# First normalisation of a two-block model: order of the loads, where the gain is applied, and how its tail interleaves with the first projections

## The reference, cut to what matters

```
h    = x * rsqrt(mean(x*x, axis=-1) + 1e-6) * attn_pre_norm     # x: 1024 x 1024
proj = h @ attn_w_in                                            # 1024 x 10240
bias = rel_bias[t5_bucket(...)]                                 # 32 x 16 table, three dilations
```

## Time and profile before

| what | value |
|---|---|
| median of 3 runs | 3475.45 us (3473.95 to 3476.17) |
| the profiled execution: its own time | 3471.2 us |
| its span, first to last instruction | 3469.0 us |
| TensorE busy, share of the span | 94% |
| VectorE, ScalarE, GpSimd busy | 43%, 33%, 31% |
| mean granted TensorE clock | 0.973 |

### The profile page before, as it was taken

One profiled execution on the slowest core, in us unless ns is written; L12 is line 12 of the kernel. 1 busy time (PEld: TensorE's weight loads), 2 busy tenths in 40 slices (PEclk: granted clock), 3 DMA queues, 4 the chain that ended last, 5 costly groups with the idle time before them and its releaser, 6 DMA issues. The chain is left out here.

```text
span 3469.0 us, 49092 instructions
## 1 busy us (share of the span) xinstructions
PE 3266.9 (94%) x19726; PEld 2605.1 (75%) x19726; DVE 1479.6 (43%) x3290; ACT 1131.0 (33%) x2453; POOL 1078.6 (31%) x541
## 2 busy tenths in 40 slices
PE   5999999999999999999999999999999899999997
PEld 4777778778787777778777777777787777777775
DVE  3253132221313236388133254455455724565554
ACT  4333434333332334321313222244342412144421
POOL 1356566222222242224332222211124122212241
PEclk8999999999999999999999999999999999999998
DMA  5313223343523323223623200101003310111113
GB/s 135 75 38 89 60 77 80 87 127 101 132 62 105 97 82 110 76 77 119 214 79 128 70 25 25 36 19 30 25 25 110 114 48 25 31 36 36 31 43 128
DMA packets 324517, 261.00 MB, mean 75 GB/s; under 512 B 75269, under 2 KB 288537, under 8 KB 324298
## 3 DMA queue, kind: packets, MB, share of 16 engines
q10 hardware_dynamic: 122156, 143.83, 13.7%
q1 hardware_dynamic: 202142, 114.09, 11.7%
HBM read 220.89 MB, written 48.58 MB: 78 GB/s over the span
## 5 line engine op out<-in xcount | busy, mean ns | idle before, releaser
L2458 POOL TENSOR_TENSOR w_hi<-w_raw,one 128x1024 fp32r<-128x1024 f32 x170 | 328.6, 1933 | 2108.8 <-PE psum L1434 1015.1
L2616 PE MATMUL psum<-act_hi,w_hi 128*128 128x512 f32 x1280 | 508.9, 398 | 31.6 <-ACT arena L1169 20.1
L1434 PE MATMUL psum<-act_hi,w_hi 128*128 128x512 f32 (+1 forms) x1376 | 511.7, 372 | 23.9 <-DVE arena L1907 13.1
L1434 PE MATMUL psum<-act_lo,w_hi 128*128 128x512 f32 (+1 forms) x1376 | 511.4, 372 | 0.0
L1434 PE MATMUL psum<-act_hi,w_lo 128*128 128x512 f32 (+1 forms) x1376 | 509.3, 370 | 0.0
L2616 PE MATMUL psum<-act_lo,w_hi 128*128 128x512 f32 x1280 | 509.0, 398 | 0.0
L2616 PE MATMUL psum<-act_hi,w_lo 128*128 128x512 f32 x1280 | 505.5, 395 | 0.0
L2461 POOL TENSOR_TENSOR w_lo<-w_raw,w_hi 128x1024 fp32r<-128x1024 f32 x170 | 432.2, 2542 | 13.3
L3364 DVE CUSTOM_DVE_ANT_0 arena<-psum,arena 128x128 f32<-128x128 f32 (+1 forms) x384 | 111.9, 347 | 506.2 <-PE psum L2655 337.6
L1434 PEld LDWEIGHTS psum<-act_hi,w_hi 128*128 128x128 f32 x1376 | 261.4, 190 | 74.6 <-DVE arena L1907 15.1
L2616 PEld LDWEIGHTS psum<-act_hi,w_hi 128*128 128x128 f32 x1280 | 242.4, 189 | 90.1 <-ACT arena L1169 22.2
(11 more groups left out here) (369 smaller groups left out, 5337.8 us busy)
## 6 DMA issues: line engine op xcount, KB each, us to landing
w_raw<-in_attn_w_in SPq DMA_DIRECT2D x80, 512.0 KB, 3.8
w_raw<-in_w_in SPq DMA_DIRECT2D x64, 512.0 KB, 4.0
spare<-in_w_mod ACTq DMA_DIRECT2D x24, 1024.0 KB, 7.9
x<-arena ACTq DMA_DIRECT2D x24, 512.0 KB, 2.9
arena<-x ACTq DMA_DIRECT2D x24, 512.0 KB, 4.4
arena<-in_x ACTq DMA_DIRECT2D x16, 512.0 KB, 5.1
arena<-weight_rows ACTq DMA_DIRECT2D x16, 512.0 KB, 6.4
w_raw<-in_ssm_w_in SPq DMA_DIRECT2D x16, 512.0 KB, 3.7
```

The lines of the kernel that those rows point to most:

```text
L1434: ins = nc.tensor.matmul(psum[:, n % 2, 0:c], w[:, slot % 2, k * P:(k + 1) * P], a[:, k, c0:c0 + c], start=(m == 0), stop=(m == 23))
L2458: G.tensor_tensor(w_hi[:, par], w_raw[:, par], one[:, 0:1].to_broadcast([P, 1024]), ALU.mult).then_inc(slot_hi, 1)
L2616: ins = nc.tensor.matmul(psum[:, h % 2, :], w[:, (3 + j) % 2, k * P:(k + 1) * P], a[:, k, c:c + 512], start=(m == 0), stop=(m == 23))
```

## The change

What it does, part by part:

1. ACT issues the first row tile before any constant, then `ident`, the gain, tile 1, `rel_bias`, `onehot`, tiles 2 and 3 in one DMA, tiles 4 and 5 in one, and after the statistics of tile 0 tiles 6 and 7 in one. All eight tiles have a buffer. An extra square root on a constant comes ahead of the first statistics.
2. The gain is loaded as a row spread over 128 partitions (512 KB), and DVE applies it with the scaling of the rows, in one instruction with two tensor inputs.
3. The turned tile is taken from PSUM directly: ACT rounds it to the high part, DVE subtracts for the low part. L255 and L290 are gone. The turned tiles lie in banks 4 to 7, the bias products in banks 0 to 2.
4. PE turns tiles 0 and 1, makes the bias products, turns tiles 2 to 4, and then puts 8 matmuls of half h = 14 ahead of each of tiles 5, 6 and 7. Then come h = 16, h = 15, and h = 17, 18, 19. The meeting of the engines is replaced by marks without a wait, and by PE's waits on `t_lo`.
5. DVE copies the bias products after scaling tile 2. SP's spread starts on that copy.
6. ACT takes out h = 14 and h = 16 ahead of `k_mat` and the bias loads. The two `c` loads, and their SiLU, are moved from the start to here: the loads behind the bias loads and ahead of the evacuations of h = 15, 17, 18 and 19, the SiLU behind those.

```diff
+        T_ROWS = region(4096, 8, 1024)
+        def start_act(act):
...
+            load(0, 1, 0)
+            act.dma_start(ident[:, :], io["c_ident"]).then_inc(const_loaded, 16)
+            act.dma_start(T_GAIN, spread_rows(io["attn_pre_norm"][0])).then_inc(const_loaded, 16)
+            load(1, 1, 1)
+            act.dma_start(relb[0:32, :], io["rel_bias"]).then_inc(const_loaded, 16)
+            act.dma_start(onehot[0:33, :], io["c_onehot"]).then_inc(const_loaded, 16)
+            load(2, 2, 2)
+            load(4, 2, 3)
+            act.wait_ge(one_set, 3)
+            nc.scalar.activation(T_STAT[:, 0, 1:2], one[:, 0:1], ACT.Sqrt)
+            stats(0)
+            load(6, 2, 0)
+            for t in range(NT):
+                if t + 1 < NT:
+                    stats(t + 1)
+                act.wait_ge(t_turned, t + 1)
+                nc.scalar.copy(act_hi[:, :, t * P:(t + 1) * P], T_PS(t % 2).rearrange("p (k c) -> p k c", k=KT)).then_inc(t_hi, 1)
...
+                if t == 0:
+                    dve.wait_ge(const_loaded, 16 * 4)
+                if t >= 2:
+                    dve.wait_ge(t_turned, t - 1)
+                nc.vector.scalar_tensor_tensor(T_NORM[:, b], T_ROWS[:, t], T_STAT[:, b, 3:4], T_GAIN,
+                                               ALU.mult, ALU.mult).then_inc(t_scaled, 1)
+            scale(0)
+            for t in range(NT):
+                if t + 1 < NT:
                     scale(t + 1)
+                if t == 1:
+                    dve.wait_ge(b_spread, 1)
+                    nc.vector.tensor_copy(spread[0:16, :, :], psum[0:16, 0:3, 0:384]).then_inc(b_copied, 1)
+                dve.wait_ge(t_hi, t + 1)
...
+                nc.vector.tensor_tensor(act_lo[:, :, cols], T_PS(t % 2).rearrange("p (k c) -> p k c", k=KT),
                                         act_hi[:, :, cols].bitcast(F32), ALU.subtract).then_inc(t_lo, 1)
...
@@ PE
             pe.wait_ge(const_loaded, 16 * 4)
+            turn_first(pe, 0)
+            turn_first(pe, 1)
...
-            t_pe(pe, 0, NT, True)
-            stage_end(pe, 1)
+            for t in range(2, 5):
+                turn_first(pe, t)
...
-            proj(-1, 14, 0, 144)
+            pe.wait_ge(b_copied, 2)
+            pe.wait_ge(t_lo, 4)
+            for i in range(3):
+                proj(-1, 14, 8 * i, 8 * i + 8)
+                turn_first(pe, 5 + i)
+            proj(-1, 14, 48, 72)
+            pe.wait_ge(t_lo, NT)
+            stage_mark(pe)
+            proj(-1, 14, 24, 48)
+            proj(-1, 14, 72, 144)
@@ ACT
+            evac(-1, 14, 0)
+            evac(-1, 16, 0)
             act.wait_ge(c_zero, 3)
             act.dma_start(k_mat[:, :, 0:P], ...).then_inc(k_stored, 16)
             act.wait_ge(b_skewed, 48)
             for g in ORDER:
                 load_bias(0, g)
-            for h in range(14, 20):
+            for i, name in enumerate(("c_2", "c_ctx_2")):
+                ...
+                act.dma_start(c_cols[:, :, i], v.rearrange("(k p) -> p k", p=P), allow_slow_non_contiguous=True).then_inc(m_c, 16)
+            for h in (15, 17, 18, 19):
                 evac(-1, h, 0)
+            act.wait_ge(m_c, 32)
+            nc.scalar.activation(c_cols[:, :, :], c_cols[:, :, :], ACT.Silu).then_inc(m_c, 1)
```

More of the change, by code:

```diff
@@ L221, in t_act @@
[L221 to L227, removed]
-            def stats(t):
[L230 to L237, removed]
+        T_ROWS = region(4096, 8, 1024)
@@ new lines, in build, with load @@
+        T_NORM = region(12288, 2, 1024)
+        T_GAIN = region(17408, 1024)
+        T_JUNK = region(18432, 1024)
+        T_STAT = region(19456, 2, 4)
+        def start_act(act):
+            tiles = x_in.rearrange("(t p) d -> p t d", p=P)
+            def load(t, n, sem_at):
+                act.dma_start(T_ROWS[:, t:t + n], tiles[:, t:t + n]).then_inc(t_loaded[sem_at], 16)
+            def stats(t):
+                b = t % 2
+                if t in (0, 1, 2, 4, 6):
+                    act.wait_ge(t_loaded[(0, 1, 2, 0, 3, 0, 0)[t]], 32 if t == 6 else 16)
+                if t >= 2:
+                    act.wait_ge(t_rstd, t - 1)
+                nc.scalar.activation(T_JUNK, T_ROWS[:, t], ACT.Square, accum_out=T_STAT[:, b, 0:1]).then_inc(t_square, 1)
+                act.wait_ge(t_square, t + 1)
@@ L238, in stats @@
                 nc.scalar.activation(T_STAT[:, b, 2:3], T_STAT[:, b, 0:1], ACT.Sqrt, scale=1.0 / D,
                                      bias=rms_eps[:, 0:1]).then_inc(t_root, 1)
[L241 to L249, removed]
-                    stats(t + 1)
[L251 to L264, removed]
@@ L266, in t_dve @@
-        def t_dve(dve, base, tiles, norm, gain, dst0):
+            load(0, 1, 0)
[6 more added lines that the diff above has]
+            load(4, 2, 3)
@@ new lines, in start_act @@
+            act.wait_ge(one_set, 3)
[4 more added lines that the diff above has]
+                if t + 1 < NT:
+                    stats(t + 1)
+                act.wait_ge(t_turned, t + 1)
+                nc.scalar.copy(act_hi[:, :, t * P:(t + 1) * P], T_PS(t % 2).rearrange("p (k c) -> p k c", k=KT)).then_inc(t_hi, 1)
+            for i in range(1, 4):
+                act.sem_inc(t_loaded[i], 16)
@@ L268, in scale, with start_dve @@
+            act.sem_inc(t_full_act, NT)
+        def start_dve(dve):
             def scale(t):
[L269 to L271 removed]
+                b = t % 2
+                dve.wait_ge(t_root, t + 1)
                 nc.vector.reciprocal(T_STAT[:, b, 3:4], T_STAT[:, b, 2:3]).then_inc(t_rstd, 1)
[L273 to L284, removed]
-                    scale(t + 1)
[L286 to L296, removed]
+                dve.wait_ge(t_rstd, t + 1)
@@ L297, in t_dve @@
                                         act_hi[:, :, cols].bitcast(F32), ALU.subtract).then_inc(t_lo, 1)
+            dve.sem_inc(t_full_dve, NT)
         def T_PS(b):
[L300 to L317, removed]
+            return psum[:, 4 + 2 * b:6 + 2 * b, :].rearrange("p a c -> p (a c)")
@@ L320, in build, with turn_first @@
+        def turn_first(pe, t):
+            pe.wait_ge(t_scaled, t + 1)
+            if t >= 2:
+                pe.wait_ge(t_lo, t - 1)
+            for k in range(KT):
+                ins = nc.tensor.transpose(T_PS(t % 2)[:, k * P:(k + 1) * P], T_NORM[:, t % 2, k * P:(k + 1) * P], ident[:, :])
+            ins.then_inc(t_turned, 1)
         PASSES = ((w_hi, act_hi), (w_hi, act_lo), (w_lo, act_hi))
@@ L2862, in _ @@
         def _(act):
[L2864 to L2875, removed]
             act.sem_inc(g_evac[0], 1)
             act.sem_inc(g_evac[1], 1)
+            start_act(act)
+            stage_mark(act)
             def load_bias(hp, g):
@@ L3337, in _ @@
             nc.vector.memset(relb[32:33, :], NEG).then_inc(b_copied, 1)
[L3338 to L3342, removed]
+            start_dve(dve)
+            stage_mark(dve)
             nc.vector.memset(BIAS[0:64, :, 576:640], NEG).then_inc(c_zero, 1)
```

18 lines of the change are left out of this document (5 added, 13 removed).

## The result

The changed kernel takes 3479.21 us (median of 20 runs, 3470.45 to 3483.97), the kernel before 3473.64 us (20 runs, 3465.44 to 3480.28). The ratio is 1.0016, 95% interval 1.0009 to 1.0023: the change costs 5.6 us (3.1 to 8.0). That is slower by 0.16%, under the 0.2% that the prediction called no change, though the interval reaches 0.23%. It is 2.2 us above the 3477.0 forecast and inside its range. The forecast stood on a kernel before of 3475.45 us (three runs); against the 3473.64 of twenty, its change of +1.5 us is to be held beside 5.6. The profiled execution took 3479.56 us, with a span of 3477.8 us and a mean granted clock of 0.972.

A forecast was written before the change was run, and what follows sets the result against it. SyncE's list, with two chokes ahead of slot 3, was taken to bound the prologue. +0.9 and +0.6 gave +1.5 us, 3471.2 to 3472.7 profiled; with the median 4.25 above, 3477.0 us, range 3472 to 3486.

The forecast's parts named there:

- The mechanism: In the prologue, SyncE's list sets the end; the norm's gain becomes a longer wait for slot 3; no change, chance 0.62.
- the head start: TensorE, after the faster norm, is 15 to 20 us ahead near 52 us; costed at nothing because slot 3 hides it.
- the chokes: Two stretches with DMA engines 5% busy, each during one `ssm_log_dt` load; forecast at 46 to 63 and 72 to 87.
- The sum: Whole prologue: +0.9 us at the first choke's start plus +0.6 for the `c` loads, together +1.5 us.
- The bias copy: DVE's copy of the bias products, which SyncE's spread awaits, ends at 20.6 us, 6.6 later (4.7 to 7.8).
- scaling tile 2 and the low part of tile 0 ... are done by 16, under the products: On DVE, both stand ahead of the bias copy but finish by 16 us, during the bias products.
- The spread no longer sharing: Row tiles 4 to 7 no longer share the DMA engines with SyncE's bias spread, saving 5.7 us.
- The `c` loads: Their 2048 single elements fall between the chokes or behind the second, costing slot 3 0 to 2 us, taken as 0.6.
- The restart: After TensorE's gap before slot 3 the clock is low as before; the longer gap changes nothing.
- the cover: TensorE finishes its sixth half near 90 us and slot 3 is ready at 96 to 97, leaving 6 to 7 us.
- The rival that put it behind the second choke: ScalarE's second `c` load is held until 86.0 us, delaying h = 15; 8.8 us lost, 3484.3 us; chance 0.28.
- The full head start: With neither ACT's queue nor slot 3 in the way, h = 17 to 19 end near 70; 26 us faster, 3449; chance 0.02.

The follow-up runs named there:

- only the late spread: Kernel before, with SyncE waiting for the high part of tile 0 before issuing the bias spread; 3478.28 us (12 runs), ratio 1.0023.
- the run with the late loads: Changed kernel, with the two `c` loads moved behind the last evacuation, h = 19; 3476.01 us (11 runs), ratio 1.0011 to the kernel before.

## Why the prediction was right, and where it was not

**The mechanism held.** SyncE's list set the end, the head start went into a longer wait for slot 3 (11.83 us, forecast longer than 5.7), the chokes lie at 46 to 64 and 73 to 88 (forecast 46 to 63 and 72 to 87), the first projection at 28.30 (forecast 28), and slot 3 is multiplied at 99.96 (forecast 97.5). TensorE was through with h = 15 at 52.84 (forecast 52). The sum was +1.5 us, with bounds of -1.3 and +4.5, and is +4.67 at the front: no change beyond 0.2% was right, the size at the front short by 3 us. That 3477.0 came within 2.2 us of the median is in part luck, since the kernel before that it was built on was 1.8 us above the median of twenty runs. The terms below are differences taken one behind the other along one path of two profiles, so they add up by construction, and a miss of 1 us in one of them is no more than two profiles of one code differ by. Term by term:

*The bias copy: +6.6 forecast, +7.3 measured.* It ends at 21.35. The constants were in at 12.0, not 10.5. DVE and TensorE around the copy:

```profile
12.02 1.28 DVE L263 SCALAR_TENSOR_TENSOR arena<-arena 128x1024 f32<-128x1024 f32 x1 [3.94 <-DMA arena<-c_onehot]
...
18.04 2.05 DVE L263 SCALAR_TENSOR_TENSOR arena<-arena 128x1024 f32<-128x1024 f32 x1
20.01 1.34 DVE L272 COPY arena<-psum 16x1152 f32<-16x1152 f32 x1
```

```profile
16.66 2.10 PE L2573 MATMUL psum<-arena 33*16 33x384 f32 x6
```

The products took 2.10 us, not 4.02, and were done at 18.76. The step that said "scaling tile 2 and the low part of tile 0 ... are done by 16, under the products" was wrong: the low part starts at 16.47, scaling tile 2 at 18.04, and the copy waits for that, not for the products. That the copy still ended only 0.7 us late is luck: the constants were 1.5 us later and DVE's order cost 1.25, and the products gave 1.9 back. The scaling itself took 2.05 us there, beside GpSimd's split of slot 1:

```profile
17.11 1.89 POOL L2430 TENSOR_TENSOR w_hi<-w_raw,one 128x1024 fp32r<-128x1024 f32 x1 [5.81 <-DMA w_raw<-in_attn_w_in]
19.09 3.23 POOL L2433 TENSOR_TENSOR w_lo<-w_raw,w_hi 128x1024 fp32r<-128x1024 f32 x1
```

Alone the two take 1.28 and 2.34 us. The Trainium skill, "SBUF — State Buffer", section "SBUF: two separate sides", says that a DVE instruction with two inputs in SBUF and a GpSimd instruction that reads SBUF exclude each other for the whole instruction. By that rule the scaling would run from 19.00 to 20.28; the trace has it end at 20.09. The low part would run from then for 2.34 us, to 22.43; it ends at 22.32. The trace agrees with the rule.

*The spread no longer sharing: -5.7 forecast, -4.4 measured.* The copy is 7.3 us later and the first `ssm_log_dt` lands 2.9 us later (66.92 against 64.01). This is the largest miss, 1.3 us, and it may be none: from the spread's first issue to that of the first `ssm_log_dt` it is 28.3 us before and 23.5 after, but 22.2 to 22.9 in the four other profiles that are the same up to there, which would be 5.4 to 6.1 us saved. The size forecast lies between.

*The `c` loads: +0.6 forecast, their cost not shown.* From the landing of the first `ssm_log_dt` to the split of slot 3 it is 28.6 us, before 27.6, and this +1.0 is what the sum needs. But with the two loads moved away it is 28.7, and in the kernel before with only the late spread, where no `c` load stands there, 28.1. What makes up the +1.0 is open.

*The restart: nothing forecast, +0.8 measured.* The clock is at 0.50 after both gaps; the step "the new gap is longer and ends the same way, so nothing changes" was wrong, four more matmuls ran slow. The length of the gap is not what did it: behind a gap of 5.29 us, in the run with only the late spread, eleven ran slow too.

The sum: 7.3 - 4.4 + 1.0 + 0.8 = 4.7 us. The norm's groups answer to the earlier trace rows:

```profile
L263 DVE SCALAR_TENSOR_TENSOR arena<-arena 128x1024 f32<-128x1024 f32 x8 | 11.0, 1380 | 4.2 <-DMA arena<-c_onehot 3.9
L275 DVE TENSOR_TENSOR act_lo<-psum,act_hi 128x1024 fp32r<-128x1024 f32 x8 | 9.8, 1219 | 4.5 <-ACT act_hi L247 4.5
```

The scaling took 1380 ns in the mean where 1.23 us were taken (1.28 but for the one beside GpSimd), and the subtraction 1219, as forecast.

**ScalarE.** It was free at 68.05 (forecast 71) and slot 3 was 2.5 us later than forecast, so the cover there was 11.8 us, not 6 to 7. The rival that put it behind the second choke (0.28) did not come true. The steps had the two `c` loads issued after the first choke. ScalarE was there sooner, held inside the first one, and freed when it ended. The run with the late loads shows what I did not know: in a choke an issue is not held as such. With `k_mat`, the bias loads and the first `c` load still under way in its queue, the issue of the second took 11.10 us; with only the first in front of it, 0.60. So what holds it is, most likely, how much of its own queue is still in front; the depth at which that begins was not measured. The rival rested on the second choke holding ScalarE. It did not where the loads came near it: in the run with the late loads they were issued as it began, and in the run with the bias copy first the second was issued in 0.61 us at 61.86, its data came at 84.0, and ScalarE went on. The Trainium skill, "DMA: Bandwidth & Descriptors", section "Issuing engines are not separate DMA queues", calls the time of issuing usually small beside the transfer. The issues of 16.03 and 11.10 us above are against it, being most of the 21.4 and 16.2 us that these two loads took to land; those of 0.38 and 0.60 us in the second choke agree with it.

**The other rivals.** The full head start was given 0.02 "were neither ACT's queue nor slot 3 in the way"; with the load mended it arrives for the most part, 21.8 of the 26 us named. As it stood, the chokes spoke against it and they decided.

## What to carry to other kernels

Before an early stage is made faster, find the last wait behind it and follow it back to the queue that ends it: 27 us of head start were worth nothing here, and the change cost 5.6, because one copy came later for it. A long issue, or a stretch where the DMA engines are 5% busy and move no bytes, names the thing to mend first. One small load with a stride of two elements kept the DMA engines near idle for 15 us or more, twice, with the transfers of two queues behind it; with it rewritten the same change gains 9 us by the medians. And when a wait vanishes in an experiment, look for it further down before counting it as won.

## What the runs showed of the hardware

- The form of one 8 KB load: `ssm_log_dt`, 64 partitions by 32 elements with a stride of two, every partition from the same addresses, kept the DMA engines at a share of 0.05 for the 15 to 17 us of a choke in the kernel before, about one engine of sixteen. Read as 64 elements in a row by 64 partitions, which is twice the bytes, it landed in 3.4 us (median of the two issues). `ssm_a_re` and `ssm_a_im`, 2048 single elements each as well, landed in 3.3 and 4.1 us right behind the mended load, so the number of single elements is not enough for a choke.
- While it ran, transfers issued behind it by SyncE and by ScalarE alike hardly moved (0 to 1 GB/s in the chokes): `k_mat`, 512 KB, took 21.5 us to land in the changed kernel, a weight slot 23.3.
- The second weight slot, issued at 1.4 us in both kernels, landed at 17.05 us where ScalarE's row tiles were issued from 0.86 us on, and at 8.37 where they came from 7.71 us on. Whether its short rows (512 bytes against 4 KB) matter was not tried.
- The same six bias products took 2.10 us right behind sixteen transposes, and 4.02 as the first work of TensorE, before and in the run with the bias copy first. The granted clock is 1.00 in all three.
- How many matmuls ran at the low clock behind the gap in front of slot 3 does not follow its length: seven behind 5.70 us (before), eleven behind 11.83 (after), eleven behind 5.29, six behind 7.59, eight behind 20.03 and ten behind 25.57 in the other runs. Why it differs was not tried.
